# A decoder layer with expert retrieval: the two softmaxes of differential attention joined by a ratio, and ScalarE's order

## The chip, the cores and the metric

The kernel runs on one core of a Trainium2 chip. The metric is device time in microseconds, from start to end of the one program. Five engines run their own instruction lists in order and wait for each other by semaphores: TensorE (PE in the profile, its weight loads PEld), VectorE (DVE), ScalarE (ACT), GpSimd (POOL) and SyncE (SP), which here only issues transfers.

## What is computed

One layer on 1024 tokens of width 1024, all in float32. The attention has 8 heads, each with two score maps, and subtracts one softmax from the other; the head's output is then normed by its root mean square over 128 values, scaled by a gain and 0.8.

```
a = probs(q1, k1) - lam * probs(q2, k2)      # softmax of q k / 8 + ALiBi bias, causal
o = a @ v
o = rms_norm(o, subln_g) * (1.0 - lam_init)  # lam_init = 0.2
merged = g_attn * (o @ w_attn_proj) + g_pool * pool_branch
h = layer_norm(DN_ALPHA * x + merged @ w_out)
# per token and each of 8 retrieval heads: 16 experts of 16384
gate = softmax(sc)                            # over the 16 best scores
act = gelu(u[idx] . h)
h = layer_norm(DN_ALPHA * h + sum(gate * act * v[idx]))
```

## The kernel before

**Tiles and stages.** The 1024 tokens are eight tiles of 128. The first half of the layer (projections, pooling, attention, branches, first norm, retrieval scores) is done for three groups of tiles: group 0 has tiles 0 and 1, group 1 tiles 2 to 4, group 2 tiles 5 to 7 (`GTS`). Group 0 runs alone, in the preamble. Groups 1 and 2 are woven into the retrieval loop of the tiles ahead of them.

**The retrieval loop.** It has 1024 slots, 128 for a tile. In each slot GpSimd gathers for every token one row of `uv` (u and v side by side, 8 KB, so 1 MB in all, L706) into one of 8 ring buffers. VectorE multiplies the u half with the token and adds up (`product`, L1306), ScalarE takes gelu of two slots together (L879), multiplies by the gate (L883) and spreads the coefficient over a diagonal (L892), and TensorE multiplies the v half by it (L1579). On many odd slots VectorE adds the v half itself (`add_row`, L1258). Then the buffer is free for the gather of eight slots later. `retrieve` finds the 16 experts of the next head a step or two per slot; ScalarE takes Exp of the gate (`exponent`, L864), VectorE divides it (`invert` and `share`, L1228 and L1233).

**A step of the attention** is one head and one tile of queries, 16 in group 0 and 24 in each of the others. TensorE makes the two score maps (L1421). VectorE adds the bias and finds the maximum (L1022, L1026). ScalarE takes Exp of both maps with their sums `den` (L782). VectorE takes the reciprocals (L1031), makes c2 = neglam / den2 (L1033), scales the second map by it (L1035), and makes the difference p_a from both (L1041): this is the mix. TensorE transposes p_a (L1440), ScalarE copies it out of PSUM as aT (L795), in chunks of up to 512 columns, chunk c of a step due a little after chunk 0. TensorE multiplies by v (L1458), VectorE copies the result to `osb` (L1053), ScalarE squares it (L805), GpSimd makes and applies the root, TensorE transposes (`outs`, L1473), and VectorE copies that with the gain `o_gain` to `o_all` (`transposed`, L1065). The root mean square norm stands between, so a factor per query matters in it only by way of its epsilon, but is kept.

**What sets the order.** Each engine has a list of streams, one for each kind of work. A stream yields the slot in which its next piece is due (a step begins at `step_at`, and the tables `DO_EXP`, `DO_ACROSS`, `DO_OT` and so on add to it). `merged` takes the earliest; of pieces due in the same slot, that of the stream named first. `woven` puts them between the slots of the loop. On ScalarE a second chunk of aT, the turned output of an earlier step (in the changed kernel) and the Exp of a later step fall due in the same slot, in groups 1 and 2, so the order of the streams in `stage` decides. The Exp of the gates is not in a stream; it is called in the loop itself, once in 16 slots. In groups 1 and 2 a score matmul waits for `o_ready`, the turned output of an earlier step, since both use the same PSUM bank, and TensorE's transpose `outs` waits for VectorE to have read the scores (`logit_done`) for the same reason.

ScalarE's functions come in tables: its list has an ACT_TABLE_LOAD wherever Exp follows gelu or gelu follows Exp.

## Time and profile before

| what | us |
|---|---|
| median of 3 runs | 3325.46 |
| lowest and highest | 3324.3, 3326.92 |
| the profiled execution, its own time | 3328.37 |
| its span | 3326.4 |
| PE busy | 2798.8 (84%) |
| DVE busy | 2475.0 (74%) |
| ACT busy | 1162.4 (35%) |
| POOL busy | 1324.7 (40%) |
| bytes moved | 1244.97 MB, mean 374 GB/s |

The first gather is issued at 297.8 us. The preamble is before it. Group 1's attention steps lie mostly in 320 to 790 us, group 2's in 1320 to 1910. A busy share says how much an engine had to do, not that it held anything up; for that a reader needs the waits in the stretch in question, and the DMA share, which is the mean of the core's 16 DMA engines. Clock 1.00 in a stretch is 2.4 GHz, the higher of TensorE's two levels, all the time.

### The profile page before, as it was taken

What the parts mean: (1) busy time and instruction counts of PE and PEld (TensorE: products, weight loads), DVE (VectorE), ACT (ScalarE), POOL (GpSimd) and SP (SyncE); (2) the same over time, 40 slices, a digit from 0 to 9 for tenths busy, and PEclk for the clock granted to TensorE, in tenths of its full rate; (3) what the DMA queues carried; (4) which work ended last, traced back from release to release, by engine and by line L of the source; (5) the groups of instructions that cost most, each with busy time, mean ns of one, the idle gap of its engine ahead of it and who ended that gap; (6) DMA issues with size and microseconds to landing.
All of it is one profiled execution on the core that took longest, in us unless ns stands there. A gap on an engine that the chain in (4) does not pass through costs nothing.

```text
span 3326.4 us, 30256 instructions
## 1 busy us (share of the span) xinstructions
PE 2798.8 (84%) x8368; PEld 1442.0 (43%) x8368; DVE 2475.0 (74%) x5989; ACT 1162.4 (35%) x3421; POOL 1324.7 (40%) x1248
## 2 busy tenths in 40 slices
PE   9999999999976799889988989867877777777776
PEld 7776565445433345444444544323433222222222
DVE  2316788896888778997799877888788676667664
ACT  2202555453122233445454522232323333333332
POOL 1101354554334343444454544344444444444432
PEclk9999999999998999999999999889989999999999
DMA  5635999999999999999999999999999999999997
GB/s 190 245 136 199 383 388 373 383 362 368 419 399 407 421 420 407 405 361 332 336 370 370 364 420 420 375 388 420 420 420 418 421 416 421 416 414 417 420 415 311
DMA packets 205223, 1244.97 MB, mean 374 GB/s; under 512 B 23680, under 2 KB 36992, under 8 KB 73600
## 3 DMA queue, kind: packets, MB, share of 16 engines
q0 software_dynamic: 147456, 1073.81, 79.8%
q1 hardware_dynamic: 56592, 169.11, 13.6%
q8 instruction: 67, 1.10, 0.1%
q14 instruction: 100, 0.82, 0.1%
q10 hardware_dynamic: 1008, 0.14, 0.0%
HBM read 1228.81 MB, written 14.16 MB: 374 GB/s over the span
## 4 chain that ended last, share of the span: by engine, by line
PE 41%; DMA 30%; DVE 18%; issue 6%; ACT 4%; POOL 1%; SPq 0%; POOLq 0%; DVEq 0%; ACTq 0%
DMA ring<-uv,idx 30%; PE r_o L1579 15%; PE w_ps L1373 14%; DVE ring L1306 8%; DVE z_e L1258 3%; PE w_ps L1421 2%; PE r_o L1550 1%; PE w_ps L1550 1%; PE w_ps L1516 1%; PE w_ps L1458 1%; PE w_ps L1493 1%; DVE e L1022 1%; POOL ring L706 1%; PE r_o L1493 1%; PE r_o L1516 1%
## 5 line engine op out<-in xcount | busy, mean ns | idle before, releaser
L706 POOL DMA_INDIRECT ring<-uv,idx x1024 | 1172.3, 1145 | 1722.9 <-PE r_o L1579 1231.0
L1579 PE MATMUL r_o<-ring,diag 128*128 128x512 f32 x2936 | 1445.6, 626 | 403.9 <-ACT diag L892 388.1
L1306 DVE CUSTOM_DVE_ANT_0 ring<-ring,ytok 128x1024 f32<-128x1024 f32 x768 | 937.1, 1221 | 234.1 <-DMA ring<-uv,idx 232.7
L1579 PEld LDWEIGHTS r_o<-ring,diag 128*128 128x128 f32 x2936 | 539.7, 195 | 1131.9 <-ACT diag L892 590.0
L879 ACT ACTIVATE gel<-dot 128x2 f32<-128x2 f32 x512 | 104.0, 203 | 1608.9 <-DVE dot L1306 1605.3
L1373 PE MATMUL w_ps<-x,w 128*128 128x384 f32 (+1 forms) x2112 | 655.4, 456 | 9.7 <-DMA x<-xT 5.9
L1373 PEld LDWEIGHTS w_ps<-x,w 128*128 128x128 f32 x2112 | 395.9, 192 | 230.0 <-issue 59.1
L1306 DVE CUSTOM_DVE_ANT_0 ring<-ring,zn 128x1024 f32<-128x1024 f32 x256 | 313.3, 1224 | 211.3 <-DMA ring<-uv,idx 211.3
L1258 DVE SCALAR_TENSOR_TENSOR z_e<-ring,coef,z_e 128x1024 f32<-128x1024 f32 x290 | 371.7, 1282 | 0.2 <-ACT coef L883 0.2
L892 ACT ACTIVATE diag<-ident,coef 128x128 f32<-128x128 f32 x734 | 262.8, 387 | 0.0
L883 ACT ACTIVATE coef<-gel,gate 128x1 f32<-128x1 f32 x1024 | 246.0, 287 | 16.8
L1550 PE MATMUL w_ps<-yT,wq 128*128 128x384 f32 x512 | 196.0, 500 | 0.6 <-ACT yT L822 0.6
L1550 PEld LDWEIGHTS w_ps<-yT,wq 128*128 128x128 f32 x512 | 100.7, 199 | 101.4 <-issue 71.8
L879 ACT ACT_TABLE_LOAD x107 | 137.3, 1283 | 1.9
L1022 DVE CUSTOM_DVE_ANT_0 e<-w_ps,bias 128x512 f32<-128x512 f32 (+3 forms) x160 | 94.5, 591 | 24.7 <-PE w_ps L1421 23.6
L1421 PE MATMUL w_ps<-k,q 64*128 64x512 f32 (+3 forms) x320 | 83.4, 599 | 31.6 <-DVE st_a L1022 20.6
L782 ACT ACTIVATE e<-e,st_a 128x384 f32<-128x384 f32 (+5 forms) x128 | 97.9, 766 | 1.2 <-DVE st_a L1026 0.7
L1458 PE MATMUL w_ps<-v,aT 128*128 128x128 f32 x528 | 73.4, 291 | 24.1 <-ACT aT L795 24.1
L1493 PE MATMUL w_ps<-o,wc 128*128 128x384 f32 x256 | 90.2, 488 | 2.7 <-DVE o L1065 2.7
L671 POOL TENSOR_SCALAR st_a<-st_a 128x1 f32<-128x1 f32 x64 | 26.2, 409 | 160.9 <-ACT junk L805 159.4
L1458 PEld LDWEIGHTS w_ps<-v,aT 128*128 128x128 f32 x528 | 69.7, 203 | 41.2 <-ACT aT L795 31.6
L1306 DVE DVE_READ_ACCUMULATOR2_ANT dot<- 128x1 f32 x1024 | 84.3, 82 | 0.0
(199 smaller groups left out, 2331.3 us busy)
## 6 DMA issues: line engine op xcount, KB each, us to landing
w<-w_in SPq DMA_DIRECT2D x132, 512.0 KB, 3.6
wq<-wq SPq DMA_DIRECT2D x46, 512.0 KB
wc<-w_branch SPq DMA_DIRECT2D x24, 768.0 KB, 8.4
ring<-uv,idx POOLq DMA_INDIRECT x1024
wo<-w_out SPq DMA_DIRECT2D x24, 512.0 KB, 10.7
xs<-x SPq DMA_DIRECT2D x8, 512.0 KB
out<-yn_e SPq DMA_DIRECT2D x8, 512.0 KB, 11.6
x<-xT SPq DMA_DIRECT2D x16, 192.0 KB, 4.0
```

The lines of the kernel that those rows point to most:

```text
L706: nc.gpsimd.indirect_dma_start(out=ring[t % RING][:], out_offset=None, in_=a["uv"], in_offset=bass.IndirectOffsetOnAxis(ap=idx[:, slot:slo ...
L879: nc.scalar.activation(gel[:, slot:slot + GROUP], dot[:, slot:slot + GROUP], ACT.Gelu).then_inc(gelu_out, 1)
L883: nc.scalar.activation(coef[:, slot + j:slot + j + 1], gel[:, slot + j:slot + j + 1], ACT.Copy, scale=gate[:, h, e_:e_ + 1]).then_inc(coef ...
L892: nc.scalar.activation(diag[u % DIAGS][:], ident[:], ACT.Copy, scale=coef[:, slot + j:slot + j + 1]).then_inc(diag_ready, 1)
L1258: nc.vector.scalar_tensor_tensor(z[:], ring[t % RING][:, D:], coef[:, slot:slot + 1], z[:], ALU.mult, ALU.add).then_inc(vsummed, 1)
L1306: nc.vector.tensor_tensor_reduce(ring[r][:, 0:D], ring[r][:, 0:D], y_of(n)[:], 1.0, 0.0, ALU.mult, ALU.add, dot[:, slot:slot + 1]).then_in ...
L1373: ins = nc.tensor.matmul(bank, w_raw[g][i % RAWS][:, c, :], x_raw[g][:, c, :], start=c == 0, stop=c == DC - 1)
L1421: nc.tensor.matmul(score_bank(g, wh)[:, 0:n], q[g][h % 2][rows, qs], keys[g][h % 2][rows, begin:begin + n], start=True, stop=True).then_in ...
L1458: ins = nc.tensor.matmul(value_bank(g)[:, 0:DV], aT[g][b // per if g else k % 2][:, b % per * P:(b % per + 1) * P], vals[g][h % 2][:, b, : ...
L1493: ins = nc.tensor.matmul(bank, branch_weights(g, n)[:, j, :], o_all[g][:, j, :], start=j == 0, stop=j == CA - 1)
L1550: ins = nc.tensor.matmul(query_bank(g)[:, 0:WS[g]], query_weights(g, i)[:, c * P:(c + 1) * P], yT[g][c // 4][:, c % 4, :], start=c == 0, s ...
L1579: ins = nc.tensor.matmul(o_ps[n % 2][half][:], diag[(u - 1) % DIAGS][:], ring[t % RING][:, D + half * HALF:D + (half + 1) * HALF], start=s ...
```

## The change

It does five things.

- The mix takes one operation over the maps less. `ratio` = neglam x den1 / den2 is a column, and p_a = e2 x ratio + e1. The factor 1/den1 that is left out is put in when the values leave PSUM: the copy to `osb` becomes a multiplication by `rden`, which is kept in four places in turn.
- The turned output's copy with its gain (`transposed`) moves from VectorE to ScalarE, with the semaphore waits it had.
- ScalarE's streams are named in another order: the aT chunks and the turned output come before Exp.
- The Exp of the gates becomes a stream too (`shares`). It falls due in the slot of an attention Exp, if one lies in the six slots from its own on (`exponent_at`); `invert` and `share` on VectorE come four slots later than before.
- ScalarE waits for a third step of the start (o_gain scaled by 0.8) before its first Exp.

```diff
+def exponent_at(g):
+
+    begin = TOPK * g - SEARCH_AHEAD + 14
+    steps = [step_at(j, k) + DO_EXP[j] for j in range(1, NG) for k in range(NSTEPS[j])]
+    return min([slot for slot in steps if begin <= slot < begin + 6], default=begin)
...
+    rden = [st_a[:, 32 + 2 * i:34 + 2 * i] for i in range(4)]
...
+        def transposed(g):
+            for k in range(NSTEPS[g]):
+                m = STEP0[g] + k
+                h, j = k // GTS[g], k % GTS[g]
+                yield step_at(g, k) + DO_OT[g] + 1
+                act.wait_ge(on_turned, m + 1)
+                if g == 1 and k == 0:
+                    act.wait_ge(q_unit, 4)
+                if g == 1 and k == GTS[g] * 4:
+                    act.wait_ge(q_unit, HP * g)
+                nc.scalar.activation(o_all[g][:, h, j * P:(j + 1) * P], out_bank(g)[:, 0:P], ACT.Copy,
+                                     scale=o_gain).then_inc(o_ready, 1)
...
-            return merged(units(g), pooling(g), exponents(g), turned_out(g), head_norm(g), first_norms(g), flipped(g),
-                          queries(g), scores_out(g))
+            return merged(units(g), pooling(g), turned_out(g), transposed(g), exponents(g), head_norm(g), first_norms(g),
+                          flipped(g), queries(g), scores_out(g))
...
+        def shares():
+            for g in range(1, RH * TT):
+                yield exponent_at(g)
+                exponent(g)
...
-        act.wait_ge(lam_step, 2)
+        act.wait_ge(lam_step, 3)
...
-        advance = woven(all_stages(stage))
+        advance = woven(merged(all_stages(stage), shares()))
...
-                ahead = SLOTS * n + slot + SEARCH_AHEAD
-                if ahead % TOPK == 14 and ahead // TOPK < RH * TT:
-                    exponent(ahead // TOPK)
...
-                nc.vector.reciprocal(rden, den).then_inc(mix_step, 1)
-                dve.wait_ge(mix_step, 3 * m + 1)
-                nc.vector.tensor_scalar(c2, rden[:, 1:2], neglam, None, ALU.mult).then_inc(mix_step, 1)
-                dve.wait_ge(mix_step, 3 * m + 2)
-                nc.vector.tensor_scalar(both[:, 1, 0:n], both[:, 1, 0:n], c2, None, ALU.mult).then_inc(mix_step, 1)
-                dve.wait_ge(mix_step, 3 * m + 3)
+                nc.vector.reciprocal(rden[m % 4], den).then_inc(mix_step, 1)
+                dve.wait_ge(mix_step, 2 * m + 1)
+                nc.vector.tensor_scalar(ratio, rden[m % 4][:, 1:2], den[:, 0:1], neglam, ALU.mult,
+                                        ALU.mult).then_inc(mix_step, 1)
+                dve.wait_ge(mix_step, 2 * m + 2)
...
-                nc.vector.scalar_tensor_tensor(p_a[g][k % 2][:, 0:n], both[:, 0, 0:n], rden[:, 0:1], both[:, 1, 0:n],
+                nc.vector.scalar_tensor_tensor(p_a[g][k % 2][:, 0:n], both[:, 1, 0:n], ratio, both[:, 0, 0:n],
                                                ALU.mult, ALU.add).then_inc(a_ready, 1)
...
-                nc.vector.tensor_copy(osb_of(g, k)[:], value_bank(g)[:, 0:DV]).then_inc(o_copied, 1)
+                nc.vector.tensor_scalar(osb_of(g, k)[:], value_bank(g)[:, 0:DV], rden[m % 4][:, 0:1], None,
+                                        ALU.mult).then_inc(o_copied, 1)
...
-                if j == 1 and 2 <= g <= RH * TT:
+                if j == 5 and 2 <= g <= RH * TT:
                     invert(g - 1)
-                if j == 2 and 2 <= g <= RH * TT:
+                if j == 6 and 2 <= g <= RH * TT:
                     share(g - 1)
```

(VectorE's `transposed`, with the same waits, is taken out, and its stream from VectorE's `stage`.)

The lists of TensorE, GpSimd and SyncE are the same in both kernels. Those of the other two differ. First ScalarE in group 2, around the coefficients of slot 392; `aT_99` is the second chunk of aT, `e_89` the maps of a step, `gate` the gate of a retrieval head, `vT` a unit of the projections. Before:

```order
L864 ACT_TABLE_LOAD
L864 ACTIVATE gate,esum<-gate 128x16
L879 ACT_TABLE_LOAD
L879 ACTIVATE gel<-dot 128x2
L883 ACTIVATE coef<-gel,gate 128x1 x2
L892 ACTIVATE diag_236<-ident,coef 128x128
L892 ACTIVATE diag_233<-ident,coef 128x128
L737 ACTIVATE vT_82<-w_ps 128x384
L782 ACT_TABLE_LOAD
L782 ACTIVATE e_89,st_a<-e_89,st_a 128x896 x2
L795 ACTIVATE aT_99<-w_ps 128x256
L879 ACT_TABLE_LOAD
```

And now, from the same gelu on (`o_123` is the turned output):

```order
L904 ACTIVATE gel<-dot 128x2
L908 ACTIVATE coef<-gel,gate 128x1 x2
L917 ACTIVATE diag_236<-ident,coef 128x128
L917 ACTIVATE diag_233<-ident,coef 128x128
L744 ACTIVATE vT_82<-w_ps 128x384
L802 ACTIVATE aT_99<-w_ps 128x256
L815 ACTIVATE o_123<-w_ps,st_a 128x128
L789 ACT_TABLE_LOAD
L789 ACTIVATE e_89,st_a<-e_89,st_a 128x896 x2
L884 ACTIVATE gate,esum<-gate 128x16
L904 ACT_TABLE_LOAD
```

The aT copy has moved ahead of Exp, the turned output stands between them, and the Exp of the gate has moved behind that of the maps, with two table loads fewer. Over the whole list ScalarE has 214 table loads before and 190 now.

Second VectorE in group 2, at a step's mix. `ISA` with `ring` and `dot` is the product of a slot, `z_e` an added row, `hot` and `rc` belong to the retrieval. Before:

```order
L1258 SCALAR_TENSOR_TENSOR z_e<-ring_222,coef,z_e 128x1024
L1209 TENSOR_TENSOR hot<-hot,topf 128x256
L1065 TENSOR_SCALAR o_123<-w_ps,st_a 128x128
L1306 ISA ring_217,dot<-ring_217,ytok_170 128x1024
L1306 ISA dot 128x1
L1213 TENSOR_REDUCE rc<-hot 128x16
L1031 RECIPROCAL st_a<-st_a 128x2
L1033 TENSOR_SCALAR st_a<-st_a 128x1
L1035 TENSOR_SCALAR e_89<-e_89,st_a 128x896
L1041 SCALAR_TENSOR_TENSOR a_93<-e_89,st_a 128x896
```

And now:

```order
L1267 SCALAR_TENSOR_TENSOR z_e<-ring_222,coef,z_e 128x1024
L1218 TENSOR_TENSOR hot<-hot,topf 128x256
L1315 ISA ring_217,dot<-ring_217,ytok_170 128x1024
L1315 ISA dot 128x1
L1222 TENSOR_REDUCE rc<-hot 128x16
L1053 RECIPROCAL st_a<-st_a 128x2
L1055 TENSOR_SCALAR st_a<-st_a 128x1
L1062 SCALAR_TENSOR_TENSOR a_93<-e_89,st_a 128x896
```

The turned output ahead of the product is gone, and so is the scaling of the map between the two columns and p_a.

## Rows read from the trace of the kernel before

**Rows 1.** Stretches: us, busy PE, PEld, DVE, ACT, POOL, clock, DMA share, GB/s
```profile
12.00:200.00 188.00, 182.33 (x896) 151.12 (x896) 55.51 (x217) 46.50 (x168) 21.98 (x48) 1.00 0.59 203
420.00:790.00 370.00, 351.40 (x1250) 198.54 (x1249) 313.55 (x787) 193.11 (x502) 183.17 (x172) 0.98 0.95 370
1320.00:1420.00 100.00, 83.76 (x267) 42.16 (x267) 90.01 (x210) 44.40 (x113) 42.54 (x40) 0.95 1.00 405
1420.00:1663.00 243.00, 215.53 (x713) 112.37 (x714) 197.68 (x491) 115.36 (x286) 104.37 (x101) 0.94 0.92 342
1663.00:1910.00 247.00, 217.04 (x764) 116.29 (x762) 225.45 (x540) 119.94 (x295) 120.42 (x110) 0.98 0.96 367
```

**Rows 2.** The same view of the gathers (L706) alone: POOL busy, in brackets how many
```profile
420.00:790.00 370.00, 129.15 (x108) 0.98 0.95 370
1420.00:1663.00 243.00, 82.44 (x70) 0.94 0.92 342
1910.00:3297.00 1387.00, 586.33 (x524) 0.96 1.01 414
```

**Rows 3.** Waits in 420:790: who waited for whom, us in total, times, longest
```profile
DVE o L1065 <- PE w_ps L1473: 26.4, 9, 6.3
...
PE w_ps L1421 <- DVE o L1065: 11.0, 6, 4.8
```

**Rows 4.** Waits in 1320:1910
```profile
PE w_ps L1458 <- ACT aT L795: 24.1, 13, 2.6
...
DVE st_a L1031 <- ACT e L782: 21.5, 18, 2.2
DVE o L1065 <- PE w_ps L1473: 20.5, 11, 4.5
PE w_ps L1421 <- DVE st_a L1022: 20.0, 12, 3.3
...
PE r_o L1579 <- ACT diag L892: 17.2, 17, 2.1
```

**Rows 5.** The chain by line, in 420:790 and in 1420:1663
```profile
by line: PE w_ps L1373 32.4%; PE r_o L1579 21.6%; DVE ring L1306 7.7%; PE r_o L1550 6.1%; DVE z_e L1258 4.9%; PE w_ps L1421 4.6%; PE w_ps L1458 3.5%; issue 3.2%; PE w_ps L1440 1.9%; DVE e L1022 1.8%; DVE a L1041 1.1%; PE r_o L1562 0.8%; DVE
by line: PE r_o L1579 23.5%; PE w_ps L1373 21.7%; DVE ring L1306 9.8%; issue 7.0%; PE w_ps L1421 5.7%; DVE z_e L1258 4.2%; PE w_ps L1458 3.7%; ACT L782 3.7%; ACT e L782 3.6%; DVE e L1022 3.1%; PE w_ps L1440 1.8%; DVE e L1035 1.1%; ACT vT L7
```

**Rows 6.** Stretches of the scaling L1035 alone: DVE busy, in brackets how many
```profile
420.00:790.00 370.00, 10.02 (x20) 0.98 0.95 370
1420.00:1663.00 243.00, 7.11 (x10) 0.94 0.92 342
```

**Rows 7.** Groups of VectorE: count, busy us, mean ns of one, idle before them
```profile
L1065 DVE TENSOR_SCALAR o<-w_ps,st_a 128x128 f32<-128x128 f32 x48 | 16.6, 346 | 47.4 <-PE w_ps L1473 47.4
L1053 DVE COPY osb<-w_ps 128x128 f32<-128x128 f32 x48 | 13.7, 286 | 16.2 <-PE w_ps L1458 16.1
```

**Rows 8.** Timeline of ScalarE in 1500:1510: start, us, engine, line
```profile
1503.21 1.28 ACT L782 ACT_TABLE_LOAD   x1
1504.51 1.04 ACT L782 ACTIVATE e<-e,st_a 128x896 f32<-128x896 f32 x1
...
1506.57 0.36 ACT L795 ACTIVATE aT<-w_ps 128x256 f32<-128x256 f32 x1
```

**Rows 9.** Groups of ScalarE, columns as in rows 7
```profile
L892 ACT ACTIVATE diag<-ident,coef 128x128 f32<-128x128 f32 x734 | 262.8, 387 | 0.0
...
L864 ACT ACT_TABLE_LOAD x63 | 80.8, 1283 | 1.1
...
L795 ACT ACTIVATE aT<-w_ps 128x512 f32<-128x512 f32 x48 | 28.1, 586 | 10.5 <-PE w_ps L1440 9.5 <-issue 1.0
...
L846 ACT ACTIVATE s<-w_ps 128x128 f32<-128x128 f32 x16 | 4.3, 267 | 11.0 <-PE w_ps L1562 11.0
```

**Rows 10.** Timeline at 662: last, the engine's idle time before it and its releaser
```profile
662.71 0.49 ACT L733 ACTIVATE k<-w_ps 128x384 f32<-128x384 f32 x1 [5.79 <-PE w_ps L1373]
662.93 0.35 DVE L1065 TENSOR_SCALAR o<-w_ps,st_a 128x128 f32<-128x128 f32 x1 [4.71 <-PE w_ps L1473]
```

21 lines of the change are left out of this document (4 added, 17 removed).

## Prediction

> **What bounds the kernel now.** I read the stretches first [rows 1]. The span divides into a preamble, in which TensorE projects and attends for the first two tiles, and the retrieval loop, in which 1024 rows of 1 MB are gathered, one a slot. Look at the DMA share. In the last stretch, 1910:3297, which holds no attention, it is 1.01, and a slot takes 1387/524 = 2.65 us [rows 1, 2]: that is the gather at its own pace, and nothing that an engine saves there comes out in the end. In the two stretches of the loop that carry attention it is lower: 0.95 in 420:790 (group 1), and 1.00, 0.92, 0.96 in 1320:1910 (group 2), and a slot takes 370/108 = 3.43 and 243/70 = 3.47 us [rows 2]. A slot there also carries weight traffic, so only the missing share can be won back: 370 x 0.06 = 22 us in group 1, and 100 x 0.01 + 243 x 0.09 + 247 x 0.05 = 35 us in group 2, **57 us** in all. That is the ceiling for anything this change does in the loop. The preamble cannot give much: TensorE is busy for 182.3 of its 188 us, and VectorE for 55.5 [rows 1].
>
> Who holds the gathers back? A row of the ring comes free when TensorE or VectorE has summed it, so I look at TensorE next. In group 1 it is busy 351.4 of 370 us, so 18.6 us are idle; the longest wait is 11.0 us (6 times) for VectorE's copy of the turned head output (L1065) before a score matmul [rows 1, 3]. In group 2 it is busy 83.8 + 215.5 + 217.0 = 516.3 of 590 us, 73.7 idle: 24.1 us (13 times) before the value matmuls for the copy aT (L795), 20.0 us (12) for VectorE to have read the scores, 17.2 us (17) for the diagonals of ScalarE [rows 1, 4]. The chain of waits says the same: in group 1 TensorE's lines lead and VectorE's product has 7.7%; in 1420:1663 the Exp of L782 and its table load have 3.6 and 3.7%, and the scaling L1035 has 1.1% [rows 5].
>
> **VectorE: what goes and what comes.** The scaling of the second exponential (L1035) goes. It takes 10.02/20 = 0.50 us a step in group 1 and 7.11/10 = 0.71 us in group 2 [rows 6]. The copy of L1065 goes, 0.346 us [rows 7]. The copy out of PSUM at L1053 (0.286 us) becomes a multiplication by a column of the same size out of the same memory, which is what L1065 was: 0.346, so +0.06 us [rows 7]. The ratio takes the place of c2, one column either way; its second pointer operand has no row, I take it at zero, and 0.1 us on 48 steps would be 5 us of VectorE, the upper bound. So VectorE loses 0.50 + 0.35 - 0.06 = 0.79 us on 24 steps of group 1, 19 us, and 0.71 + 0.35 - 0.06 = 1.00 us on 24 steps of group 2, 24 us. Its wait for TensorE's transpose goes too, but a wait is not work, and the paragraph on the cost shows where it goes. VectorE is 90 and 91% busy in 1320:1420 and 1663:1910 and 81 to 85% elsewhere [rows 1].
>
> **ScalarE: the order.** Three things happen at the place where a step's Exp stands. First, the aT copy that falls due with it now goes ahead of it. In the trace the two Exp with their table load start at 1503.21 and the aT copy at 1506.57 [rows 8]: so the value matmuls, which need it, can start 3.36 us later than they could. The 24.1 us that TensorE waits for aT in group 2 [rows 4] are of this kind. The new order takes them away; what is next late is VectorE's reading of the scores and the diagonals, on the same engine's list, so I count half: **12 us**, with 4 and 24 as bounds. Group 1 has this copy in one step of three and no such wait among its longest, so nothing.
> Second, the turned output copy comes to ScalarE, directly ahead of Exp. No row has this operation. A copy of this size from PSUM without a pointer takes 0.267 us, one from SBUF with a pointer 0.387 [rows 9]; the scaled one has the pointer of the second, so I take 0.37, 24 us for 64, of which VectorE's 22 us were the mirror. Third, the Exp of a retrieval's gate now stands next to an attention Exp where one is near, and the list of ScalarE has 190 table loads where it had 214: 24 x 1.283 us [rows 9] = 31 us less. ScalarE is therefore some 7 us lighter in all, on an engine that is 44 to 52% busy there [rows 1].
>
> The cost: Exp comes later by the two copies in front of it, 0.37 us in group 1 (0.63 in every third step) and 0.37 + 0.48 = 0.85 us in group 2, with the aT copies of 256 to 512 columns at 0.36 [rows 8] to 0.59 us [rows 9]. VectorE waits for Exp in the trace (21.5 us in 18 times in group 2 [rows 4]), and where it does, the missing scaling gives 0.71 back: +0.14 us a step in group 2, -0.05 in group 1. So **for the path Exp, mix, turn the change is about even**, and the 43 us of VectorE are worth something only where VectorE was late for another reason. The example is at 663 [rows 10]: VectorE idles 4.71 us before L1065, ScalarE 5.79 us before the copy of k, both for TensorE; afterwards VectorE makes its product early and then waits for the same Exp. That wait moves, it doesn't go.
>
> **The sum.** Group 2: 12 us for aT; 24 us of VectorE at the share that VectorE has on the chain there, some 25% (its product 9.8%, its row sum 4.2%, its score reading 3.1%, small ones the rest [rows 5]), 6 us; Exp later where VectorE waits, -2 us; fewer table loads between diagonals, of whose 17.2 us I take 2. Together 18 us of at most 35. Group 1: VectorE's 19 us at 17% (7.7 + 4.9 + 1.8 and small ones [rows 5]), 3 us; the 11.0 us wait for L1065, which ScalarE now ends, but from a queue in which a unit's copy stands ahead, a third, 4 us; Exp, zero. Together 7 us, but TensorE has only 18.6 idle, so I take 5. The preamble: VectorE and ScalarE are covered by TensorE, 0 (between -2 and +2). The gate's reciprocal and share, moved four slots on, have until the head's first coefficient: 0. In all 18 + 5 = 23 us, which I lower to **20**, since the gathers share their queues with weight loads whose times move too. The profiled execution took 3328.4 us, 2.0 more than its span, and would take 3308; the median of the runs is 3325.5, and 20 less is **3305.5 us**.
>
> At the reload the notes and the rows differ. The Trainium skill (ScalarE: Activation LUTs, What ACT_TABLE_LOAD costs) gives "~1283 ns" for the load and adds a drain of 1380, 2.66 us for each switch. The load agrees with the rows; the drain does not appear: Exp starts at 1504.51, 1.30 us after its load began at 1503.21 [rows 8]. By the page the 24 loads would be 64 us and the half of the aT waits some 5 us more, with 3300 as the result; I go by the row.
> The same page (Rules for kernel authors) says to use VectorE, not ScalarE, for a multiplication, which speaks against moving L1065. The nearest rows give 0.27 to 0.39 against 0.346 us, so the move itself is about even and its worth is a matter of queues.
>
> **The rivals.** *The stretches fill up* (12%): the aT wait goes whole and VectorE's relief lets the ring run ahead, so most of the missing DMA share comes back: 40 to 57 us, 3268 to 3285. For it: TensorE's 73.7 idle us in group 2. Against it: TensorE is 95% busy in group 1.
> *Hidden* (17%): the waits only change hands, as at 663; TensorE waits for the scores' reader where it waited for aT. 0 to 7 us, 3319 to 3325. For it: in the example ScalarE and VectorE are released within 0.22 us of each other, by TensorE [rows 10], whatever stands first on either.
> *ScalarE waits in front of Exp* (8%), the slower side: the turned output must be transposed on TensorE before ScalarE gets past it to Exp and to the next gelu. If TensorE's transpose comes late, Exp, the mix and all coefficients of the next slots stand behind it. VectorE waited 26.4 us in 9 times for that transpose in group 1 and 20.5 in 11 in group 2 [rows 3, 4]. In the trace ScalarE stood mostly behind another copy until then; if it did not, and each of the 47 us reached the end, less the 20 won, this would be 3352. It decides from about 20 us of new wait on the path; half of it gives 3329.
> *It does not do what it says*: the lists show that it does, so only in that the loads saved lie outside the attention stretches, which is in the "hidden" case.
>
> **Chances.** My forecast, 7 to 40 us less, 63%; filling up 12%; hidden 17%, of which some is above 6.7 us; slower 8%. A measurement tells about 0.2%, 6.7 us, from no change. Faster by more: 0.77; within: 0.16; slower: 0.07. The range leaves out the far half of the filling case and the slow one: 3280 to 3324.
>
> **What would show it.** Right: the wait of the value matmuls for aT in group 2 falls from 24 us to under 6; VectorE is busy some 50 us less in all; 24 table loads fewer; DMA share 0.95 or more in the stretch that had 0.92; the last stretch keeps 2.65 us a slot. VectorE's wait for Exp rises above the 21.5 us. Wrong: a wait of ScalarE for the transpose of over 20 us in the loop; gelu waiting less for VectorE while TensorE waits more for the diagonals; a preamble that is longer by over 2 us.

## The result, and the profile after

The changed kernel takes 3331.78 us, median of 22 runs (3322.59 to 3336.53), against 3325.31 us for the kernel before in 22 runs beside it (3320.49 to 3328.44). The ratio is **1.0019** with a 95% interval of 1.0012 to 1.0025: 6 us slower, just within the 0.2% that the prediction called no change, where 20 us less was forecast. The prediction was wrong; the time lies outside its range of 3280 to 3324 us.

In what follows a ratio is always against the kernel before, run on the same chip; 0.1% is 3.3 us. Microseconds for a ratio are the ratio less one, times 3325; they can differ by some 3 us from the difference of the medians.

The profiled run of the changed kernel took 3328.67 us (span 3326.7), 3 us under its median, so its trace shows a little less than the whole loss. First the engines' busy time from its page, then the stretches, with the columns of rows 1:

```profile
PE 2811.2 (85%) x8368; PEld 1447.5 (44%) x8368; DVE 2430.9 (73%) x5861; ACT 1149.1 (35%) x3461; POOL 1320.9 (40%) x1248
```

```profile
420.00:790.00 370.00, 353.38 (x1267) 199.96 (x1266) 307.46 (x764) 190.12 (x522) 191.40 (x176) 1.00 0.96 376
1320.00:1420.00 100.00, 83.67 (x267) 41.54 (x266) 89.77 (x214) 42.65 (x113) 41.54 (x38) 0.92 1.00 405
1420.00:1663.00 243.00, 213.22 (x716) 110.94 (x716) 187.61 (x464) 110.20 (x290) 95.79 (x101) 0.95 0.92 342
1663.00:1910.00 247.00, 216.74 (x754) 116.87 (x753) 210.63 (x506) 113.52 (x295) 116.86 (x107) 0.95 0.93 356
```

The work went away as intended: VectorE is busy 44.1 us less (2475.0 before), ScalarE 13.3 us less (1162.4 before). But in 1420:1663 the DMA share, against [rows 1], stands at 0.92 as before, and in 1663:1910 it has fallen from 0.96 to 0.93. The gathers alone (L713, columns of rows 2) say where the change gained and where it lost:

```profile
420.00:790.00 370.00, 134.19 (x110) 1.00 0.96 376
1320.00:1910.00 590.00, 214.47 (x175) 0.95 0.94 358
1910.00:3200.00 1290.00, 552.25 (x487) 0.94 1.01 415
```

Group 1 issues 110 gathers where it issued 108 [rows 2]; at 3.43 us a slot that is a gain of some 7 us. One execution can't carry that figure, though: run e14 below has the changed kernel's lists up to group 2, and its own row is that of 108 gathers again:

```profile
420.00:790.00 370.00, 132.16 (x108) 0.98 0.95 372
```

Group 2 issues 175 in 1320:1910, and the kernel before 180 in the same stretch. The last stretch runs at 1290/487 = 2.65 us a slot, as [rows 2]. So the loss is made in group 2. To compare the same work there, take the stretch from the first of its 24 turned outputs to the last (columns of rows 1). The kernel before, then the changed one:

```profile
1404.07:1936.13 532.06, 462.81 (x1558) 242.60 (x1559) 458.07 (x1106) 249.49 (x624) 247.02 (x232) 0.96 0.94 360
1400.19:1940.60 540.41, 466.15 (x1558) 244.27 (x1559) 440.30 (x1070) 241.13 (x634) 242.29 (x232) 0.94 0.93 355
```

With the same 1558 matmuls on record it takes 8.3 us longer. TensorE is idle 74.3 us instead of 69.3, and busy 3.3 us longer, at a granted clock of 0.94 instead of 0.96. The waits of group 2, in 1320:1910, as [rows 4]:

```profile
DVE st_a L1053 <- ACT e L789: 59.4, 21, 5.5
PE r_o L1588 <- ACT diag L917: 31.9, 15, 3.8
PE w_ps L1449 <- issue: 19.5, 9, 4.7
PE w_ps L1430 <- DVE st_a L1044: 18.1, 8, 3.2
ACT o L815 <- PE w_ps L1482: 6.1, 5, 1.9
```

TensorE's wait for aT, 24.1 us before [rows 4], is gone. In its place stands a wait of the next transposes (L1449, L1440 before), 5.0 us before and 19.5 now; the wait for the diagonals has grown from 17.2 to 31.9 us, and VectorE's for Exp from 21.5 to 59.4 [rows 4]. Part of the last is no loss: VectorE no longer waits 20.5 us for the turned output [rows 4], and comes to Exp earlier. The releaser "issue" is no answer: the profile didn't find who ended that wait. The code tells it. `turn_bank` and `value_bank` are the same PSUM bank, so the transposes wait for `o_copied`, VectorE's copy of the values to `osb`.

Last the groups that the prediction had priced (columns as in rows 7):

```profile
L904 ACT ACT_TABLE_LOAD x95 | 121.9, 1283 | 1.7
L1055 DVE TENSOR_SCALAR st_a<-st_a 128x1 f32<-128x1 f32 x64 | 17.5, 273 | 2.3
L815 ACT ACTIVATE o<-w_ps,st_a 128x128 f32<-128x128 f32 x48 | 17.4, 362 | 16.1 <-PE w_ps L1482 16.1
L1074 DVE TENSOR_SCALAR osb<-w_ps,st_a 128x128 f32<-128x128 f32 x48 | 16.6, 346 | 28.3 <-PE w_ps L1467 27.1 <-issue 1.1
```

### The profile page after: what moved, and what is told of

The parts are those of the page before. It is cut to its first block, busy times and chain, and to the rows that moved or that the text cites. A ratio compares the mean times of both kernels' runs of the same rounds, so it can differ in the third digit from the quotient of the medians.

```text
span 3326.7 us, 30168 instructions
## 1 busy us (share of the span) xinstructions
PE 2811.2 (85%) x8368; PEld 1447.5 (44%) x8368; DVE 2430.9 (73%) x5861; ACT 1149.1 (35%) x3461; POOL 1320.9 (40%) x1248
## 3 DMA queue, kind: packets, MB, share of 16 engines
q0 software_dynamic: 147456, 1073.81, 79.8%
q1 hardware_dynamic: 56592, 169.11, 13.5%
## 4 chain that ended last, share of the span: by engine, by line
PE 42%; DMA 30%; DVE 16%; issue 6%; ACT 5%; POOL 1%; SPq 0%; POOLq 0%; DVEq 0%
DMA ring<-uv,idx 30%; PE r_o L1588 15%; PE w_ps L1382 15%; DVE ring L1315 7%; DVE z_e L1267 3%; PE w_ps L1430 2%; PE r_o L1559 1%; PE w_ps L1559 1%; PE w_ps L1525 1%; ACT e L789 1%; POOL ring L713 1%; PE w_ps L1467 1%; PE r_o L1502 1%; PE r_o L1525 1%; ACT diag L917 1%
## 5 line engine op out<-in xcount | busy, mean ns | idle before, releaser
L713 POOL DMA_INDIRECT ring<-uv,idx x1024 | 1180.9, 1153 | 1729.4 <-PE r_o L1588 1273.7
L1588 PE MATMUL r_o<-ring,diag 128*128 128x512 f32 x2936 | 1462.1, 632 | 409.5 <-ACT diag L917 398.5
L1053 DVE RECIPROCAL st_a<-st_a 128x2 f32<-128x2 f32 x64 | 10.5, 164 | 150.0 <-ACT e L789 149.9
```

Source lines behind the costliest of these rows:

```text
L713: nc.gpsimd.indirect_dma_start(out=ring[t % RING][:], out_offset=None, in_=a["uv"], in_offset=bass.IndirectOffsetOnAxis(ap=idx[:, slot:slo ...
L1588: ins = nc.tensor.matmul(o_ps[n % 2][half][:], diag[(u - 1) % DIAGS][:], ring[t % RING][:, D + half * HALF:D + (half + 1) * HALF], start=s ...
```

## One place, read closely

I took one step of group 2, around 1430 us, at which a second chunk of aT falls due with Exp. TensorE's list there is the same in every kernel below: turned output of an earlier step, value matmuls (12, which need the second chunk of aT), four score matmuls, four transposes of the next p_a. Rows of the timeline (start, us, engine, line; in brackets the idle time before and its releaser). The kernel before:

```profile
1431.35 0.27 PE L1473 MATMUL w_ps<-ident,osb 128*128 128x128 f32 x1
...
1431.55 0.49 ACT L737 ACTIVATE vT<-w_ps 128x384 f32<-128x384 f32 x1 [2.75 <-PE w_ps L1373]
...
1432.06 1.28 ACT L782 ACT_TABLE_LOAD   x1
...
1435.42 0.36 ACT L795 ACTIVATE aT<-w_ps 128x256 f32<-128x256 f32 x1
1435.55 0.17 DVE L1031 RECIPROCAL st_a<-st_a 128x2 f32<-128x2 f32 x1 [2.06 <-ACT e L782]
...
1435.83 2.50 PE L1458 MATMUL w_ps<-v,aT 128*128 128x128 f32 x12 [2.16 <-ACT aT L795]
...
1440.46 0.28 DVE L1053 COPY osb<-w_ps 128x128 f32<-128x128 f32 x1
...
1440.85 0.41 PE L1440 MATMUL w_ps<-ident,a 128*128 128x128 f32 x2 [0.74 <-issue]
```

And the kernel before with nothing but aT moved ahead of Exp (run e7 below):

```profile
1428.52 0.27 PE L1473 MATMUL w_ps<-ident,osb 128*128 128x128 f32 x1
...
1429.11 0.38 ACT L795 ACTIVATE aT<-w_ps 128x256 f32<-128x256 f32 x1
1429.50 1.28 ACT L782 ACT_TABLE_LOAD   x1
1430.80 1.04 ACT L782 ACTIVATE e<-e,st_a 128x896 f32<-128x896 f32 x1
...
1430.67 1.50 PE L1458 MATMUL w_ps<-v,aT 128*128 128x128 f32 x12
...
1432.99 0.17 DVE L1031 RECIPROCAL st_a<-st_a 128x2 f32<-128x2 f32 x1 [2.34 <-ACT e L782]
...
1437.91 0.28 DVE L1053 COPY osb<-w_ps 128x128 f32<-128x128 f32 x1
...
1438.29 0.44 PE L1440 MATMUL w_ps<-ident,a 128*128 128x128 f32 x1 [5.06 <-issue]
```

Count from the turned output. The value matmuls come 4.48 us after it before and 2.15 us after it in e7, and they start without a wait: that is the gain that was forecast. Yet the transposes come 9.50 us after it before and **9.77** in e7. Between the values and the copy of them to `osb` lie, on VectorE's list, the mix, a product, an added row and a step of the retrieval, and the mix waits for Exp. From the mix's first operation (L1031) to the transposes it is 1440.85 - 1435.55 = 5.30 us before and 1438.29 - 1432.99 = 5.30 us in e7. So the transposes follow the mix, the mix follows Exp, and Exp has come 0.27 us later. At this place the values were never what TensorE waited for in the end.

I call this span, from the turned output's start to the transposes' start, the **loop of the place**. The same span one step earlier, 1404.08 to 1415.75 in the kernel before, is 11.67 or 11.68 us in each of the 20 kernels of the table, so a hundredth can be read. The table has it beside each ratio. "24 x" is the change of the loop against the kernel before, for 24 steps. "group 2" is the change of the stretch from the first to the last turned output of group 2, 532.1 us before.

| run | edit | ratio, 95% | us | loop | 24 x | group 2 |
|---|---|---|---|---|---|---|
| before | | 1 | | 9.50 | |  |
| e6 | ratio alone | 0.9957 (0.9943 to 0.9970) | -14 | 8.90 | -14 | -11 |
| e7 | aT ahead of Exp alone | 1.0031 (1.0019 to 1.0044) | +10 | 9.77 | +6 | +8 |
| e5 | both | 0.9987 (0.9978 to 0.9996) | -4 | 9.16 | -8 | 0 |
| e2 | changed, turned output on VectorE | 0.9993 (0.9984 to 1.0002) | -2 | 9.17 | -8 | -2 |
| e3 | changed, gate's Exp in the loop | 0.9990 (0.9980 to 0.9999) | -3 | 9.43 | -2 | +2 |
| e8 | the same, its division still late | 0.9998 (0.9989 to 1.0007) | -1 | 9.42 | -2 | +5 |
| after | the whole change | 1.0019 (1.0012 to 1.0025) | +6 | 9.43 | -2 | +8 |
| e4 | changed, without the ratio | 1.0053 (1.0040 to 1.0066) | +18 | 10.03 | +13 | +11 |
| e12 | e6, spare copies after Exp | 0.9971 (0.9960 to 0.9982) | -10 | 9.16 | -8 | -4 |
| e11 | e6, spare copies before Exp | 0.9986 (0.9977 to 0.9994) | -5 | 9.35 | -4 | +1 |
| e9 | e5, osb copy ahead of the mix | 1.0030 (1.0018 to 1.0041) | +10 | 6.19 | -79 | +16 |
| e16 | Exp first of all, no ratio | 0.9972 (0.9962 to 0.9983) | -9 | 7.35 | -52 | -8 |
| e10 | e6, Exp first of all | 0.9936 (0.9923 to 0.9949) | -21 | 7.34 | -52 | -15 |
| e13 | e10 and the merged gate's Exp | 0.9940 (0.9927 to 0.9954) | -20 | 6.75 | -66 | -21 |
| e14 | changed, Exp first in group 2 | 0.9928 (0.9915 to 0.9942) | -24 | 7.54 | -47 | -24 |
| e15 | e14, gate's Exp in the loop | 0.9926 (0.9912 to 0.9939) | -25 | 7.34 | -52 | -24 |
| e18 | e15, Exp a slot earlier | 0.9923 (0.9909 to 0.9937) | -26 | 4.65 | -116 | -19 |
| e17 | e15, group 1 reordered too | 0.9909 (0.9894 to 0.9924) | -30 | 5.65 | -92 | -21 |
| e1 | changed, Exp ahead of aT and turned output | 1.0084 (1.0064 to 1.0103) | +28 | 8.89 | -15 | -1 |

For changes of up to some 0.6 us, 24 times the loop gives the time within 8 us, mostly within 5 (e1, which lost in group 1, apart). That is in part luck, since the other places don't repeat it. Summed over the 21 turned outputs of group 2 that transposes follow, the loops change by -4.7 us in e6, +3.4 in e7 and +10.1 in the changed kernel, and in e7 single ones move between -1.8 and +2.9. Larger cuts bring much less than 24 times themselves. So the loop shows how one place works and is no model of the whole. The last column is the better measure: it follows the time within 10 us in every row but e1.

## Experiment 1: the five edits one by one

**e6, the ratio alone** (the changed mix, `rden` in four places and the multiplication at `osb`; ScalarE's order, gate and turned output as before), and **e4, the changed kernel without it**.

```diff
-                nc.vector.tensor_scalar(c2, rden[:, 1:2], neglam, None, ALU.mult).then_inc(mix_step, 1)
-                dve.wait_ge(mix_step, 3 * m + 2)
-                nc.vector.tensor_scalar(both[:, 1, 0:n], both[:, 1, 0:n], c2, None, ALU.mult).then_inc(mix_step, 1)
-                dve.wait_ge(mix_step, 3 * m + 3)
+                nc.vector.tensor_scalar(ratio, rden[m % 4][:, 1:2], den[:, 0:1], neglam, ALU.mult,
+                                        ALU.mult).then_inc(mix_step, 1)
+                dve.wait_ge(mix_step, 2 * m + 2)
```

> The kernel before with the ratio alone (Exp ahead of the aT chunk as before). Theory D: the ratio gives 11 us anywhere, 3312 to 3316. The prediction's own step, that the ratio's gain on the path Exp, mix, turn is real and the aT order is worth 12 us more: 3316 to 3320, and e5 some 12 us below it. Theory B (waits only change hands): within 3 us of 3325.

> The changed kernel with the mix as it was (the second map scaled, then joined, and a plain copy out of PSUM), everything else changed. Theory A: the path Exp, mix, turn is 0.5 to 0.7 us a step longer on 48 steps, so 3342 to 3358. Theory B: within 3 us of 3332.

Measured: 0.9957 alone, 14 us less; 1.0053 against 1.0019 where it is taken out of the changed kernel, 11 us more. So the ratio is good in both orders. The loop of the place shortens by 0.60 us: 0.69 for the scaling that goes, less 0.273 - 0.214 = 0.06 for the column with two pointers [L1055 above; L1033 before] and small changes between operations. The stretch of group 2 in e6:

```profile
1401.28:1922.20 520.92, 457.31 (x1558) 240.00 (x1559) 446.78 (x1093) 250.87 (x624) 258.44 (x232) 0.96 0.96 368
```

It is 11.1 us shorter: TensorE is idle 5.6 us less and busy 5.5 less. That the length of the mix pays, which lies between Exp and the transposes, and not VectorE's load, is argued and not tested by itself. For it speaks e2 below: with the turned output back on VectorE, 17 us more load, the kernel is faster and not slower.

**e7, aT ahead of Exp alone**, and **e5, the ratio with it**. One line in either, on ScalarE:

```diff
-            return merged(units(g), pooling(g), exponents(g), turned_out(g), head_norm(g), first_norms(g), flipped(g),
+            return merged(units(g), pooling(g), turned_out(g), exponents(g), head_norm(g), first_norms(g), flipped(g),
                           queries(g), scores_out(g))
```

> The kernel before with one edit: the aT chunk goes ahead of Exp when both fall due together. The prediction's step: the 24 us in which TensorE waits for aT in 1320 to 1910 go, and 12 us with them, so 3311 to 3315. Theory B: they go, and as much comes back before the diagonals and the transposes of p_a, 3322 to 3328.

> The changed kernel with two parts undone: the turned output's copy on VectorE and the gate's Exp in the loop (reciprocal and share at their old slots). What is left is the ratio and the aT chunk ahead of Exp. Theory D (the parts add: the ratio gives 11 us, the turned output on ScalarE costs 9 and the merged gate Exp 9): 3309 to 3316, the fastest so far. Theory E (the two costs are one, since both lengthen the same stretch of ScalarE between two gelus, so undoing one has already got it back): 3318 to 3324.

Measured: 1.0031 alone; on top of the ratio 0.9987 against 0.9957. Both times it costs 0.3%, 10 us, where I had counted a gain of 12. The waits of e7 in 1320:1910, of TensorE and VectorE:

```profile
DVE st_a L1031 <- ACT e L782: 28.1, 19, 2.5
PE r_o L1579 <- ACT diag L892: 27.9, 17, 3.3
...
PE w_ps L1440 <- issue: 23.6, 10, 5.1
```

The 24.1 us for aT [rows 4] have become 18.6 us more before the transposes (5.0 in 7 times before), 10.7 more before the diagonals (17.2 in 17) and 6.6 more before the mix (21.5 in 18). This one line accounts for the larger part of what TensorE's waits in the changed kernel show, not of VectorE's.

The waits are half of the loss. The same stretch in e7, from turned output to turned output, and behind it a piece of it at the place:

```profile
1402.94:1943.01 540.07, 466.88 (x1558) 244.08 (x1559) 459.03 (x1114) 250.53 (x624) 247.63 (x232) 0.94 0.94 356
1436.75:1443.50 6.75, 5.21 (x10) 2.85 (x11) 6.75 (x15) 2.99 (x11) 1.37 (x2) 0.50 0.70 250
```

Of its 8.0 us more, 3.9 are idle time and 4.1 are a TensorE that is busy longer with the same matmuls: the clock is 0.94 for 0.96, and the mean matmul of the v halves (L1579) takes 661 ns instead of 630 (652 in the changed kernel). At the place the clock stands at its lower level, 0.50 or 1.2 GHz, for 6.8 us, within which TensorE's wait of 5.1 us ends; in the kernel before it stood there for 3.4 us, from 1436.3 on, after a wait of 2.2 us. In that stretch the clock is 0.935 to 0.947 in the eight kernels that have aT ahead of Exp in group 2, and 0.948 to 0.966 in the others, but for e1 (0.926). So the lower clock comes with that order; that the longer waits bring it fits these rows, but no run changes the clock alone.

**e2, the turned output back on VectorE**, **e3, the gate's Exp back in the loop with its division four slots earlier**, **e8, the Exp back and the division late**, each taken from the changed kernel.

```diff
-            return merged(units(g), pooling(g), turned_out(g), transposed(g), exponents(g), head_norm(g), first_norms(g),
+            return merged(units(g), pooling(g), turned_out(g), exponents(g), head_norm(g), first_norms(g),
                           flipped(g), queries(g), scores_out(g))
...
-            return merged(pooling(g), logits(g), outputs(g), branches(g), residuals(g), first_norms(g))
+            return merged(pooling(g), logits(g), outputs(g), transposed(g), branches(g), residuals(g), first_norms(g))
```

```diff
-        advance = woven(merged(all_stages(stage), shares()))
+        advance = woven(all_stages(stage))
...
+                ahead = SLOTS * n + slot + SEARCH_AHEAD
+                if ahead % TOPK == 14 and ahead // TOPK < RH * TT:
+                    exponent(ahead // TOPK)
```

> The changed kernel with the turned output's copy back on VectorE, the aT chunk still ahead of Exp. Theory A: Exp starts some 0.4 us earlier and no longer behind TensorE's transpose, but VectorE has 22 us more work and its wait for the transpose again: 3322 to 3330. Theory C (the move to ScalarE is what costs, since ScalarE stands behind the transpose): back to 3325 or below. Theory B: within 3 us of 3332.

> The changed kernel with the gate's Exp called in the loop again, once in 16 slots, and VectorE's reciprocal and share at their old slots: 214 table loads instead of 190. If the saved loads are worth something: 3335 to 3345. Theory B: within 3 us of 3332. If the merged Exp costs (longer stay in the Exp table before the next gelu): 3320 to 3328.

> The changed kernel with the gate's Exp in the loop again, but VectorE's reciprocal and share left at the later slots (5 and 6). It parts e3's gain: if the later slots on VectorE were the cost, 3329 to 3334 as in the changed kernel; if it was the Exp's place on ScalarE, 3318 to 3324 as in e3.

Measured: 0.9993, 0.9990 and 0.9998, against 1.0019 with everything and 0.9987 (e5) with neither. So of the turned output's move and the gate's merging each one alone costs nothing that can be told (+0.03 and +0.06%), and the two together 0.3%. The turned output makes the loop 0.26 us longer (9.43 against 9.17), which the ratio and aT left at -0.33. What makes the pair dearer than its parts I can't show. The division's time is at most a small part of it: e8 and e3 overlap. It is gone where Exp stands first (e14 and e15 below). It isn't at the place that I read either: the 21 loops together change by +3.1 us in e2, +3.2 in e3 and +10.1 in the changed kernel, but also by +6.7 in e8, which isn't slow. **It stays open**, and it is some 8 us of the result (0.32% less 0.03 and 0.06).

## Experiment 2: is it Exp's start?

My theory after these was: group 2's time hangs on when Exp starts on ScalarE, whatever stands ahead of it. The rival: ScalarE's load as such, or the copies' own lateness. **e11** puts four spare copies of 32 columns, which no one reads, before each of the 24 Exp of group 2, behind Exp's own wait, **e12** the same four behind it, both in e6.

```diff
+                if g == NG - 1:
+                    for i in range(4):
+                        nc.scalar.activation(junk[g][:, 32 * i:32 * i + 32], ident[:, 32 * i:32 * i + 32], ACT.Copy)
                 for wh in range(2):
```

> e6 with four spare copies of 32 columns on ScalarE ahead of Exp in the 24 steps of group 2, some 0.55 us a step, 13 us in all, as long as the aT chunk is. Their output is read by nobody. Theory F: all of it is paid, 3321 to 3326, as e5 against e6. Theory G (the aT chunk's early end is what costs, by the work that it lets TensorE do sooner): 3311 to 3315.

> The same four spare copies behind Exp, ahead of the aT chunk. The stretch of ScalarE between two gelus is as long as in e11, Exp is not late. Theory F: 3311 to 3316. Theory H (the length of that stretch counts, through the diagonals): as e11, 3321 to 3326.

The 96 copies are busy for 13.8 us in e11, 0.57 us a step:

```profile
L790 ACT ACTIVATE junk<-ident 128x32 f32<-128x32 f32 x96 | 13.8, 216 | 4.4 <-DVE st_a L1041 4.4
```

Measured: ahead of Exp they cost 0.29% on e6, 10 us of 14; behind it 0.14%, 5 us. The intervals of the two touch (0.9977 to 0.9994 and 0.9960 to 0.9982), and that of e12 overlaps that of e6 (0.9943 to 0.9970). So the cost ahead of Exp is clear of noise; the cost behind it and the difference are not quite. The loop of the place says the same: +0.45 us ahead, +0.26 behind, 24 times which are 11 and 6 us. In 1320:1910 VectorE waits 30.9 us for Exp in e11, 21.5 in e12 and 20.9 in e6; TensorE waits for aT 30.7, 29.9 and 23.8 us. So what stands ahead of Exp costs about three quarters of its length; what stands behind is probably not free either, as aT then comes later. Moving aT across takes its length from one and gives it to the other, the dearer, so by these figures it couldn't win. They give a loss of some 5 us, half of the 10 of e7; the rest of that isn't shown by them.

**e9** tries the other end of the chain: if the transposes wait for the copy to `osb` behind the mix, put that copy ahead of the mix (in e5).

```diff
-DO_OSB = (12, 12, 14)
+DO_OSB = (12, 12, 12.9)
```

> e5 (ratio, aT chunk ahead of Exp) with one edit: in group 2 VectorE's copy of the values out of PSUM stands ahead of the mix of the next step, in the same slot, not one slot and a product behind it. Theory F (TensorE's next transposes wait for that copy, since both use one PSUM bank, and that copy waits behind the mix, so an earlier aT gains nothing and a later Exp costs all it is late): the wait of the transposes, 17 us in 1320 to 1910, falls under 6, and the time from e5's 3320 to 3302 to 3312. Theory B: within 3 us of 3320.

Measured: 1.0030, 14 us slower than e5 (0.9987). The transposes' wait with the releaser "issue", 17.5 us in e5, isn't among the waits any more (5.5 us for p_a stand there), and the loop is 3 us shorter. But VectorE now waits for the values. In 1320:1910, VectorE of e9:

```profile
DVE osb L1064 <- PE w_ps L1470: 59.6, 20, 8.6
```

Behind that wait stand the products and, behind those, ScalarE's coefficients: TensorE's wait for the diagonals is 44.5 us in 28 times, against 31.4 in 17 in e5. The mechanism is confirmed (the transposes did wait for that copy) and the remedy is worse than the wait. It also shows that a short loop at one place is no proof of a fast kernel.

## Experiment 3: Exp ahead of everything

**e1** was my first try: the changed kernel with Exp ahead of aT and of the turned output in all groups.

```diff
-            return merged(units(g), pooling(g), turned_out(g), transposed(g), exponents(g), head_norm(g), first_norms(g),
+            return merged(units(g), pooling(g), exponents(g), turned_out(g), transposed(g), head_norm(g), first_norms(g),
```

> The changed kernel with one part undone: on ScalarE the Exp of the maps comes ahead of the aT chunk and of the turned output again, which both stay behind it. Theory A (Exp is late: in the changed kernel VectorE waits 150 us for Exp where it waited 82, and this eats what the ratio saved): the wait falls under 100 us and the time to 3310 to 3322. Theory B (TensorE and the queues set the pace of the attention stretches, and a saved wait only changes hands): within 3 us of the changed kernel's 3332, and TensorE's wait for aT comes back (24 us).

Measured: 1.0084 (1.0064 to 1.0103), 28 us slower. Its trace splits it. The gathers of e1:

```profile
420.00:790.00 370.00, 120.05 (x99) 0.95 0.91 345
1320.00:1910.00 590.00, 216.15 (x180) 0.94 0.96 368
```

Group 2 is back at 180, so there the order of before is better, as e7 has it. Group 1 lost 11 gathers of 110. Its waits in 420:790:

```profile
PE w_ps L1430 <- ACT o L815: 36.2, 15, 5.0
```

In the changed kernel that wait is 8.3 us in 5 times. The granted clock is 0.95 there and 1.00 in the changed kernel, and the matmuls are slower as well (330.6 us busy for 1155, against 353.4 for 1267). In group 1 the score matmuls need the bank of the turned output, and once ScalarE makes that copy behind Exp, TensorE stands still. So the turned output must stay ahead of Exp in group 1 and not in group 2.

**e10** (e6 with Exp ahead of the projection copies too, which the kernel before has in front), **e13** (e10 with the merged gate's Exp) and **e16** (the kernel before with that order alone; the turned output is VectorE's in all three):

```diff
-            return merged(units(g), pooling(g), exponents(g), turned_out(g), head_norm(g), first_norms(g),
+            return merged(exponents(g), units(g), pooling(g), turned_out(g), head_norm(g), first_norms(g),
```

> e6 (ratio alone, 3311) with Exp named first of ScalarE's streams, so that it no longer waits behind a projection's copy that falls due with it. Theory F: Exp starts up to 3 us earlier in two steps of three, 3296 to 3307. Against it: the projections' copy comes 4 us later and holds up TensorE's next unit, in the preamble too: 3315 to 3330.

> e10 (ratio, Exp first of ScalarE's streams, 3304) with the gate's Exp merged as in the changed kernel, 190 table loads. If the merge costs by itself: 3310 to 3316. If it costs only together with the turned output on ScalarE: 3301 to 3307. If the 24 loads saved (31 us of ScalarE) are worth something once Exp is early: 3295 to 3301.

> The kernel before with one edit, Exp first of ScalarE's streams; no ratio. Theory F: the 7 us between e6 and e10 are there without the ratio too, 3315 to 3320. If Exp's place is worth something only with the shorter mix: 3322 to 3328.

Measured: 0.9936, 0.9940 and 0.9972. The order alone is worth 0.28%, the ratio alone 0.43%, both 0.64%. Merging the gate's Exp does nothing here that can be told.

**e14** is the changed kernel, whole, with Exp first in group 2 only:

```diff
         def stage(g):
+            if g == NG - 1:
+                return merged(exponents(g), units(g), pooling(g), turned_out(g), transposed(g), head_norm(g), first_norms(g),
+                              flipped(g), queries(g), scores_out(g))
             return merged(units(g), pooling(g), turned_out(g), transposed(g), exponents(g), head_norm(g), first_norms(g),
```

> The changed kernel with ScalarE's streams in another order in group 2 alone: Exp first, then the projections' copies, aT and the turned output. Group 1 keeps the changed order. Theory F (Exp's start sets the pace of group 2, and e1 was slow in group 1 alone, where the score matmuls wait for the turned output): 20 to 25 us under the changed kernel, 3307 to 3314. If e1's loss lay in group 2 as well: 3335 and more.

Measured: 0.9928 (0.9915 to 0.9942), 24 us under the kernel before and 30 under the changed one, from another order of the same streams in one group. Its stretches, to be held against those above:

```profile
1420.00:1663.00 243.00, 221.58 (x767) 115.34 (x767) 202.89 (x499) 119.41 (x314) 114.88 (x110) 0.98 0.96 365
1663.00:1910.00 247.00, 216.60 (x735) 114.81 (x735) 220.39 (x517) 112.79 (x300) 126.03 (x114) 0.95 0.98 389
```

The DMA share rises from 0.92 and 0.93 to 0.96 and 0.98. And the place at 1430:

```profile
1428.14 1.28 ACT L789 ACT_TABLE_LOAD   x1
...
1428.79 0.27 PE L1485 MATMUL w_ps<-ident,osb 128*128 128x128 f32 x1
...
1431.63 0.17 DVE L1056 RECIPROCAL st_a<-st_a 128x2 f32<-128x2 f32 x1 [1.54 <-ACT e L789]
...
1431.87 0.37 ACT L802 ACTIVATE aT<-w_ps 128x256 f32<-128x256 f32 x1
...
1432.40 1.50 PE L1470 MATMUL w_ps<-v,aT 128*128 128x128 f32 x12
...
1435.88 0.34 DVE L1077 TENSOR_SCALAR osb<-w_ps,st_a 128x128 f32<-128x128 f32 x1
...
1436.33 0.41 PE L1452 MATMUL w_ps<-ident,a 128*128 128x128 f32 x2 [1.36 <-issue]
```

The table load starts 0.65 us ahead of the turned output, 0.71 behind it in the kernel before. There ScalarE stood idle 2.75 us for the unit's copy `vT`, with Exp behind it. So in the earlier orders an operation whose inputs were there stood behind one that waited for TensorE. The mix to the transposes is 1436.33 - 1431.63 = 4.70 us, the 5.30 of before less the ratio's 0.60, and the aT wait comes back in small: 12.0 us in 6 times.

Three variants: **e15** takes the merged gate's Exp out again, **e17** also puts the turned output and Exp first in groups 0 and 1, **e18** lets e15's Exp fall due one slot earlier in group 2.

```diff
-            return merged(units(g), pooling(g), turned_out(g), transposed(g), exponents(g), head_norm(g), first_norms(g),
+            return merged(transposed(g), exponents(g), units(g), pooling(g), turned_out(g), head_norm(g), first_norms(g),
```

```diff
-DO_EXP = (3, 5, 5)
+DO_EXP = (3, 5, 4)
```

> e14 with the gate's Exp in the loop again (214 loads). If gate Exp and turned output cost together because both lengthen what stands around Exp: 7 to 11 us under e14. If that cost was there only while Exp stood behind the turned output: within 4 us of e14.

> e15 with groups 0 and 1 reordered as well: the turned output and then Exp are named ahead of the projections' copies, so that Exp is earlier there and no score matmul waits longer for the turned output. Theory F for group 1: its 24 steps are VectorE-paced too, 3288 to 3296. If TensorE, 95% busy there, is the limit of group 1: 3296 to 3302.

> e15 with Exp due one slot earlier in group 2, in the slot in which VectorE finds the maximum. Theory F without a limit (the earlier the better): 3290 to 3296. If ScalarE then stands in front of Exp waiting for VectorE, and the gelus with it: 3302 to 3315.

Measured: 0.9926, 0.9909 and 0.9923. e15 and e18 can't be told from e14. e18's loop is 4.65 us, 2.7 less than e15's, and its time the same: from there on a shorter loop at this place is no longer what counts. e17 has the lowest median of all, 3296.78 us in 4 runs, 28 us under the median of the kernel before (30 by the ratio); its interval (0.9894 to 0.9924) overlaps that of e15. Its gathers in both groups:

```profile
420.00:790.00 370.00, 140.89 (x114) 1.00 0.97 379
1320.00:1910.00 590.00, 224.82 (x186) 0.95 0.97 378
```

In group 1 that is 114 against 113 in e15 and 110 in the changed kernel. The DMA share is now 0.97 in both. Reckoned as the prediction did, 370 x 0.04 + 590 x 0.04 = 38 us of its 57 are still missing there, so the ceiling isn't reached.

## Why the prediction was wrong

**What bounds the kernel, and the ceiling: right.** The last stretch keeps 2.65 us a slot, what is won or lost is the missing DMA share of the attention stretches, and the best version wins 30 us, inside the 57. The 3 us taken off the sum because "the gathers share their queues with weight loads" rest on nothing in the profile: its page of the kernel before has 1073.81 MB in queue q0, which is the 1024 gathers, and 169.11 MB in q1, the weights among them; what they share is the 16 DMA engines.

**VectorE's load: right in size, wrong in use.** 43 us of busy time were forecast to go (the list of signs said some 50), 44.1 went. The multiplication at `osb` takes 0.346 us, as priced from L1065; the column with two pointers 0.273 against 0.214, inside the bound of 0.1. But I turned that time into path time by VectorE's share of the chain, 25%, 9 us (6 and 3) for the ratio and the turned output's move together. The ratio alone brings 14. At the place read it is 0.60 us shorter on the chain Exp, mix, copy, transposes.

**aT first, 12 us: the step that failed.** The forecast missed by 26 us (-20 against +6); this term missed by 22 (-12 against +10), more than any other. I read the 24.1 us of [rows 4] as TensorE's loss and halved it, naming "VectorE's reading of the scores and the diagonals" as next late. Next late was, before either, what the sum had not named: the transposes behind the values, waiting for VectorE's copy behind the mix behind Exp. Measured alone it is +10 us (e7), the same on top of the ratio (e5 against e6). The diagonals were late too, 27.9 us in e7 for 17.2. And the sum kept TensorE's matmuls at their length, where they took 4.1 us more in group 2 at a lower clock. The bounds of 4 to 24 us gain had the wrong sign at both ends; below nothing was not considered, although the paragraph on the cost moved Exp back by the copy's length.

**"For the path Exp, mix, turn about even": right at the place, and not carried into the sum.** I had 0.85 us of copies against 0.71 saved, +0.14 us a step. The loop of the place gives +0.27 for aT, +0.26 for the turned output, -0.60 for the ratio, together 9.43 against 9.50, -0.07. Had I let this path alone decide, group 2 would have come out 3 us slower by my own +0.14, 2 us faster by the measured -0.07; it took 8.3 us longer. I added three gains beside it (12, 6 and 2), of which the first and the last were not found in any run.

**The turned output and the gate's Exp: the second miss.** The sum had them as gains, 4 us for the wait for L1065 and 2 for the table loads. Measured together on top of the ratio and aT they cost 0.32%, 11 us (the changed kernel against e5). Against the forecast this is 17 us the wrong way. Two things hide part of it: the ratio brings 14 us where VectorE's terms less the later Exp had 7, and I had lowered the sum by 5 us (2 in group 1, 3 at the end). 22 + 17 - 7 - 5 is 27, the 26 but for rounding.

**ScalarE: right in size.** The turned output takes 0.362 us (0.37 forecast), 24 table loads are gone, ScalarE is 13 us lighter (7 forecast). The lighter ScalarE brought nothing: merging the gate's Exp is within the uncertainty in e2 against e5, in e13 against e10 and in e14 against e15, and costs 0.3% in the changed kernel against e3. In the rows of e7 above, Exp of the load at 1429.50 starts at 1430.80, 1.30 us later, as it did in [rows 8], and the load starts 0.01 us after aT's copy ends. The drain of 1380 ns that the Trainium skill adds (ScalarE: Activation LUTs, What ACT_TABLE_LOAD costs) appears in neither. The time of the whole kernel can't decide on it: e15, which brings the 24 loads back, agrees with e14 within 0.02%, so the loads aren't on the path at either price.

**Group 1, 5 us: not contradicted.** Its stretch issues two gathers more, some 7 us, but e14 with the same lists there issues none more. The preamble was to change by at most 2 us; the first gather is issued at 295.6 us, 2.2 earlier, and in e14 at 297.8, as in the kernel before. Group 2, forecast at 18 us less, took 8.3 us more; the two profiled runs as wholes take the same time within 0.3 us, and by the medians the changed kernel takes 6 us more.

**The rivals.** *Hidden* had the kind of mechanism right, waits that change hands (TensorE's idle time in group 2 changes by 5 us, where 24 us for aT went), and its range of 3319 to 3325 us missed by 7 us since it allowed no loss. *ScalarE waits in front of Exp* had the sign, at 8%, by another mechanism: ScalarE waits 6.1 us for the transpose of the turned output in group 2 and 10.1 in group 1, not 20 and more. Of the signs listed, the aT wait under 6 us, the 24 loads, the last stretch and the longer Exp wait came true; the DMA share of 0.95 in the 0.92 stretch did not, and that was the one that counts. Of the signs of being wrong one came: in 1320:1910 gelu waits less for VectorE (216.3 us, 220.1 before) while TensorE waits more for the diagonals (31.9 and 17.2).

**What is left.** Step by step the runs go from the kernel before to the changed one: -0.43% for the ratio (e6), +0.30% for aT (e5), +0.32% for the turned output and the gate's Exp together, in all +0.19%. Of the last step each part alone costs 1 to 2 us, within noise. The other 8 us, the joint cost, have no cause that the runs settle (e2, e3 and e8). Nor is it shown what the lower clock would have cost without the longer waits.

## What to carry to other kernels

A wait in the table isn't a loss until you have followed the waiting engine's list past it: ask what the operation behind it waits for, and on which chain that lies. Here 24 us of waiting for aT were slack behind the cycle Exp, mix, copy, transposes. An edit that shortened that cycle by 0.6 us at the place read gave 14 us, and one that took the wait away at Exp's expense cost 10. Look at the granted clock as well: with the waits moved, the same matmuls took 4 us longer. In an in-order list put the operation whose inputs are ready and whose result starts the longest chain ahead of those that wait for another engine: the order of the streams in one group turned a change that lost 0.2% into one that gains 0.7%.

## What the runs showed that was not expected

- A wait with the releaser "issue" can be a wait for a PSUM bank: the transposes' 5.06 us ended 0.38 us after VectorE's copy to `osb` began, in the kernel before 0.39 us after it, and the wait vanished when that copy was moved (e9).
- A copy of 128x32 on ScalarE from SBUF takes 0.216 us, one of 128x128 out of PSUM 0.267 [rows 9]: between these two the number of operations counts more than their size.
- A second pointer operand, with the multiplication by it, on a one-column operation of VectorE costs 0.06 us (0.273 against 0.214).
- TensorE's granted clock in group 2 went with ScalarE's order: 0.935 to 0.947 in the eight kernels with aT ahead of Exp, 0.948 to 0.966 in the others but e1.
